# Value pages in four slots, three rounding slots, ranking in PSUM and the key ring over other buffers in a hybrid DeltaNet and MoBA step

## The reference

```
kp = cache_k[i, page_table].reshape(db, past_len, MOBA_HEADS, HEAD_DIM)
gate = jnp.einsum('bhtd,bhnd->bhtn', qh, k_mean)          # k_mean: mean key of each block of 256
_, sel = lax.top_k(gate, n_sel)                            # the best 3 blocks, and the own one
logits = einsum(q, k) * scale - slopes * dist              # ALiBi; others are -1e30
p = softmax(logits); out = einsum(p, v)
```

## Time and profile before

| | |
|---|---|
| median of 3 runs | 1305.23 us (1303.71 to 1305.43) |
| the profiled execution | 1302.96 us, its span 1301.2 us |
| PE busy | 1143.8 us, 88% of the span |
| DVE, ACT, POOL busy | 722.9, 563.0, 294.1 us |
| granted clock of TensorE, mean | 0.937 |
| DMA | 182.62 MB, 140 GB/s over the span |

### The profile page before, as it was taken

The page is one execution under the profiler, slowest core; times in us unless marked ns, Lnnn a source line. Parts: engine busy times, 40 slices in busy tenths (PEclk is TensorE's granted clock), DMA queues, the critical chain, the costliest instruction groups (busy, mean ns, idle before and its releaser), DMA issues.

```text
span 1301.2 us, 20535 instructions
## 1 busy us (share of the span) xinstructions
PE 1143.8 (88%) x7143; PEld 1005.1 (77%) x7143; DVE 722.9 (56%) x1216; ACT 563.0 (43%) x886; POOL 294.1 (23%) x262
## 2 busy tenths in 40 slices
PE   5999689778788788767989999997999799999995
PEld 4999689455455454443889999996999699999994
DVE  4743624566656766642466666345556566666333
ACT  3447301344454555433364444335334554443434
POOL 8201015101454554453220000022101310000011
PEclk9999959888989999985989999998999899999997
DMA  7334100335657666735425345343444244544421
GB/s 229 114 103 157 35 1 1 119 133 186 210 196 242 226 207 215 246 110 162 135 85 174 129 139 181 116 134 118 129 153 149 95 130 147 175 129 135 151 78 40
DMA packets 119124, 182.62 MB, mean 140 GB/s; under 512 B 6128, under 2 KB 59471, under 8 KB 118990
## 3 DMA queue, kind: packets, MB, share of 16 engines
q1 hardware_dynamic: 116274, 173.30, 40.6%
q0 software_dynamic: 2784, 8.47, 2.4%
HBM read 176.12 MB, written 5.63 MB: 140 GB/s over the span
## 4 chain that ended last, share of the span: by engine, by line
PE 46%; ACT 3%; DVE 2%; POOL 1%; issue 0%; DVEq 0%; POOLq 0%
PE bank L1618 46%; POOL xl L617 1%; ACT xres L953 1%; DVE xres L1068 1%; ACT hi L674 1%; ACT xh L674 1%; PE bank L2015 0%; ACT L944 0%; PE bank L2083 0%; DVE xres L1480 0%; DVE hraw L1068 0%; PE bank L2005 0%; DVE lo L1061 0%; DVE lnt L1068 0%; ACT lnt L946 0%
## 5 line engine op out<-in xcount | busy, mean ns | idle before, releaser
L1618 PE MATMUL bank<-xh,hi 128*128 128x320 f32 x1184 | 373.7, 316 | 40.0 <-POOL xl L617 26.4
L1618 PE MATMUL bank<-xl,hi 128*128 128x320 f32 x1184 | 371.3, 314 | 0.0
L1618 PE MATMUL bank<-xh,lo 128*128 128x320 f32 x1184 | 370.9, 313 | 0.0
L1061 DVE TENSOR_TENSOR lo<-raw,hi 128x2048 fp32r<-128x2048 f32 x102 | 241.3, 2366 | 188.6 <-ACT hi L674 188.6
L1618 PEld LDWEIGHTS bank<-xh,hi 128*128 128x128 f32 x1184 | 227.5, 192 | 43.1 <-issue 31.2
L674 ACT ACTIVATE hi<-raw 128x2048 fp32r (+1 forms) x102 | 194.8, 1909 | 107.6 <-PE bank L1618 107.6
L1618 PEld LDWEIGHTS bank<-xl,hi 128*128 128x128 f32 x1184 | 227.5, 192 | 0.1
L1618 PEld LDWEIGHTS bank<-xh,lo 128*128 128x128 f32 x1184 | 227.2, 192 | 0.0
L594 POOL TENSOR_TENSOR lo<-vring,hi 128x1024 fp32r<-128x1024 f32 x60 | 145.0, 2418 | 176.1 <-ACT hi L674 176.0
L1068 DVE TENSOR_TENSOR kTl<-bank,kTh 128x512 fp32r<-128x512 f32 x128 | 88.1, 689 | 103.6 <-ACT kTh L674 101.6
L1618 PE MATMUL bank<-hh,hi 128*128 128x320 f32 x416 | 129.3, 311 | 1.3 <-DVE hraw L1068 1.3
(11 more groups left out here) (376 smaller groups left out, 1500.1 us busy)
## 6 DMA issues: line engine op xcount, KB each, us to landing
raw<-w_up SPq DMA_DIRECT2D x44, 1024.0 KB
kring<-cache_k SPq DMA_DIRECT2D x128, 256.0 KB, 3.7
vring<-cache_v SPq DMA_DIRECT2D x128, 256.0 KB, 3.4
raw<-w_down SPq DMA_DIRECT2D x8, 2048.0 KB
raw<-w_in_mix SPq DMA_DIRECT2D x7, 2048.0 KB
raw<-w_in_sc SPq DMA_DIRECT2D x8, 1024.0 KB
raw<-w_down SPq DMA_DIRECT2D x4, 1536.0 KB
raw<-w_out_mix SPq DMA_DIRECT2D x2, 2048.0 KB
```

The source lines that it names most:

```text
L1061: dve.tensor_tensor(lo[:, p], weight(n)[:, :, 256 * p:256 * p + 256], hi[:, p], ALU.subtract)\
L1618: return pe.matmul(out, lhsT, rhs, start=start, stop=stop, **kw)
```

## The change

- `vring` has four slots of two pages in place of two of four. SP waits and loads by pairs of pages (`load_pair`), two pairs behind each key group; a pair may be loaded when the unit four back has its low part. The number of transfers and of table words is the same.
- Three rounding slots instead of two: `vxh`, `vxl` lie over `kvtok`, the prompt's keys and values, once these are stored. `ROUND_V` is one or two steps earlier. POOL makes all low parts of samples 0 to 6, DVE all of sample 7.
- In the ranking, the block sums are copied into PSUM, and ties, ranks and penalties are kept there; `rk` alone stays in SBUF. Four copies of block maxima become additions with a penalty operand in PSUM.
- The copying of queries and their low part go from DVE to POOL, samples 0 and 1 ahead of the loop.
- `kring` lies over DeltaNet buffers that are dead earlier. SP waits for PE's step o1 and DVE's qg2 for the first group and PE's stS2 for the second, instead of stS3. The first group goes to slot 1.
- Of the four sums for the DeltaNet norm and their logarithms two move into step 0; the prompt's stages move by a step (its values on PE stay at step 13).
- The table `keyb` is made in four operations over 128 partitions, during the inversion, from a small table `spread`, instead of sixteen in step 2 of sample 0.
- `split_lo(S_OUT, 0)` goes from (8, 5) to (7, 11) in DVE's program. The filler stays at (8, 1).

The core of the diff:

```diff
-        c128 = sb("c128", [32, 128], stack=sA)
+        c128 = sb("c128", [P, 128], stack=sA)
         back = sb("back", [32, NPG + 1], stack=sA)
         slope = sb("slope", [32, 1], stack=sA)
         ownb = sb("ownb", [32, 120], stack=sA)
+        keyb = sb("keyb", [P, 512], stack=sA)
+        spread = sb("spread", [P, 5], stack=sA)
...
-        vring = sb("vring", [P, 2, 4, 512], stack=s3)
+        vring = sb("vring", [P, 4, 2, 512], stack=s3)
...
+        kring = sb("kring", [P, 2, 4, 512], stack=s3)
...
+        vxh = sb("vxh", [P, 2, 512], F32R, stack=s3)
+        vxl = sb("vxl", [P, 2, 512], F32R, stack=s3)
...
-        PROMPT = {1: "kv0", 3: "scores", 5: "kv1", 10: "turn", 13: "values"}
+        PROMPT = {0: "sums", 1: "kv0", 4: "scores", 6: "kv1", 11: "turn", 13: "values"}
...
-        ROUND_V = {5: (1, 0), 7: (1, 1), 9: (1, 2), 11: (1, 3), 13: (1, 4), 15: (1, 5), 1: (2, 6), 3: (2, 7)}
-
-        def lo_by_dve(n):
-
-            return n >= VALL - VUNITS and n % 2 == 1
-
-        def lo_ready(eng, n):
-
-            dve_made = sum(lo_by_dve(i) for i in range(n + 1))
-            after(eng, "v_lo", n + 1 - dve_made)
-            after(eng, "v_lo_dve", dve_made)
+        ROUND_V = {3: (1, 0), 5: (1, 1), 8: (1, 2), 10: (1, 3), 12: (1, 4), 14: (1, 5), 0: (2, 6), 2: (2, 7)}
+        LAST_V = VALL - VUNITS
+        vhs = [vh[:, 0], vh[:, 1], vxh[:, :, :]]
+        vls = [vl[:, 0], vl[:, 1], vxl[:, :, :]]
+
+        own_b, pTown_b, den_b = bank[7][0:32, 0:SMP], bank[7][0:SMP, 64:96], bank[7][0:SMP, 96:100]
+        gm_b, tie_b, rank_b, pen_b = (bank[7][0:32, i:i + n] for i, n in
+                                      ((128, NBLK), (136, NBLK * NBLK), (200, NBLK), (208, NBLK)))
...
-            DV.wait(sp_, "stS3")
-            AC.wait(sp_, "oT1")
...
-            def load_pages(ring, cache, landed, n):
-                words = [sp_.value_load(pair[0:1, 2 * n + j:2 * n + j + 1], min_val=0, max_val=POOL * POOL - 1)
-                         for j in range(2)]
-                for j, w in enumerate(words):
-                    for u, x in enumerate((w % POOL, w // POOL)):
-                        sp_.dma_start(ring[:, n % 2, 2 * j + u, :], cache[bass.ds(x, 1)].rearrange("o p h d -> (o p) (h d)"))\
-                           .then_inc(s[f"{landed}{n % 2}"], 16)
+            def load_pair(out, cache, landed, n):
+                w = sp_.value_load(pair[0:1, n:n + 1], min_val=0, max_val=POOL * POOL - 1)
+                for u, x in enumerate((w % POOL, w // POOL)):
+                    sp_.dma_start(out[:, u, :], cache[bass.ds(x, 1)].rearrange("o p h d -> (o p) (h d)")).then_inc(s[landed], 16)
 
             for n in range(4 * NB + 5):
+                if n == 0:
+                    PE.wait(sp_, "o1")
+                    DV.wait(sp_, "qg2")
+                if n == 1:
+                    PE.wait(sp_, "stS2")
                 if n < 4 * NB:
                     after(sp_, "kT_mm", 4 * n - 4)
-                    load_pages(kring, a["cache_k"][0], "k_in", n)
+                    x = (n + 1) % 2
+                    load_pair(kring[:, x, 0:2], a["cache_k"][0], f"k_in{x}", 2 * n)
+                    load_pair(kring[:, x, 2:4], a["cache_k"][0], f"k_in{x}", 2 * n + 1)
                 if n == 5:
                     PE.wait(sp_, "po1")
-                if n >= 5:
-                    lo_ready(sp_, 2 * (n - 5) - 3)
-                    load_pages(vring, a["cache_v"][0], "v_in", n - 5)
+                for m in (2 * n - 10, 2 * n - 9):
+                    if m >= 0:
+                        after(sp_, "v_lo", m - 3)
+                        load_pair(vring[:, m % 4], a["cache_v"][0], f"v_in{m % 4}", m)
...
+            def queries(b):
+                after(pool, "own_mm", b - 1)
+                after(pool, "s_mm", UNITS * (b - 1))
+                pool.tensor_copy(qpf[:, b % 2, :].rearrange("p (h r) -> p h r", r=40)[:, :, 0:NT],
+                                 mbh[:, 0:H, SEQ + NT * b:SEQ + NT * b + NT]).then_inc(s["q_fp"], 1)
+
+            def queries_lo(b):
+                pool.wait_ge(s["q_hi"], b + 1)
+                pool.tensor_tensor(qpl[:, b % 2, :], qpf[:, b % 2, 0:128], qph[:, b % 2, :], ALU.subtract).then_inc(s["q_lo"], 1)
+
+            DV.wait(pool, "rowc")
+            for b in range(2):
+                queries(b)
+                queries_lo(b)
...
-                if lo_by_dve(n):
-                    continue
-                w = n % 2
+            for n in range(LAST_V):
                 pool.wait_ge(s["v_hi"], n + 1)
-                pool.tensor_tensor(vl[:, w], vring[:, n // 2 % 2, 2 * w:2 * w + 2, :], vh[:, w], ALU.subtract)\
-                    .then_inc(s["v_lo"], 1)
+                pool.tensor_tensor(vls[n % 3], vring[:, n % 4], vhs[n % 3], ALU.subtract).then_inc(s["v_lo"], 1)
+                b = n // VUNITS + 2
+                if b < NB and n % VUNITS == 2:
+                    queries(b)
+                if b < NB and n % VUNITS == 4:
+                    queries_lo(b)
...
+            def o_logs(hs):
+                for h in hs:
+                    PE.wait(act, f"oss{h}")
+                    AC.up(act.activation(qg[:, h, :], bank[6 + h % 2][:, 0:TOK], ACT.Ln, scale=1.0 / HD, bias=eps6[:, 0:1]),
+                          f"oln{h}")
...
+                    o_logs((2, 3))
+                    act.preload_act_table(ACT.Exp)
...
-                act.wait_ge(s[f"v_in{n // 2 % 2}"], 64 * (n // 4 + 1))
-                after(act, "v_mm", n - 1)
-                copy(vh[:, n % 2], vring[:, n // 2 % 2, 2 * (n % 2):2 * (n % 2) + 2, :]).then_inc(s["v_hi"], 1)
+                act.wait_ge(s[f"v_in{n % 4}"], 32 * (n // 4 + 1))
+                after(act, "v_mm", n - 2)
+                if n == 2:
+                    act.wait_ge(s["stores"], 16 * 11)
+                copy(vhs[n % 3], vring[:, n % 4]).then_inc(s["v_hi"], 1)
...
+                    for g in range(4):
+                        dve.tensor_copy(spread[32 * g:32 * g + 32, 0:4], back[:, 4 * g:4 * g + 4])
+                        ins = dve.tensor_copy(spread[32 * g:32 * g + 32, 4:5], slope[:, 0:1])
+                    DV.up(ins, "spread")
+                    DV.wait(dve, "spread")
+                    for i in range(4):
+                        dve.tensor_scalar(keyb[:, PAGE * i:PAGE * i + PAGE], c128[:, :], spread[:, i:i + 1], spread[:, 4:5],
+                                          ALU.subtract, ALU.mult)
...
-                    for g in range(NPG):
-                        ins = dve.tensor_scalar(keyb[32 * (g // 4):32 * (g // 4) + 32, PAGE * (g % 4):PAGE * (g % 4) + PAGE],
-                                                c128[:, :], back[:, g:g + 1], slope[:, 0:1], ALU.subtract, ALU.mult)
-                    DV.up(ins, "keyb")
...
-            def queries(b):
-                after(dve, "own_mm", b - 1)
-                for h in range(H):
-                    ins = dve.tensor_copy(qpf[:, b % 2, h, NT * h:NT * h + NT],
-                                          mb[:, TOK * h + SEQ + NT * b:TOK * h + SEQ + NT * b + NT])
-                ins.then_inc(s["q_fp"], 1)
-
-            def queries_lo(b):
-                dve.wait_ge(s["q_hi"], b + 1)
-                tt(qpl[:, b % 2], qpf[:, b % 2], qph[:, b % 2], ALU.subtract).then_inc(s["q_lo"], 1)
...
-                link(dve.tensor_reduce(bm[:, :], sbias[:, c % 2, 0:512].rearrange("p (n k) -> p n k", n=2), AX.X, ALU.max))
+                dve.tensor_reduce(bm[:, :], sbias[:, c % 2, 0:512].rearrange("p (n k) -> p n k", n=2), AX.X, ALU.max)
+                dve.wait_ge(s["summed"], 4 * c + 4)
+                link(dve.tensor_copy(gm_b, gsum[:, :]))
+
+            def ranks(c):
+
+                wins = rk[:, :].rearrange("p (n m) -> p n m", m=NBLK)
+                ties = tie_b.rearrange("p (n m) -> p n m", m=NBLK)
+                gm, gn = mid(gm_b, NBLK), last(gsum[:, :], NBLK)
+                tt(wins, gm, gn, ALU.is_gt)
+                link(tt(ties, gm, gn, ALU.is_equal))
+                link(tt(ties, ties, ltri[:, :, :], ALU.mult))
+                link(tt(wins, ties, wins, ALU.add))
+                link(dve.tensor_reduce(rank_b, wins, AX.X, ALU.add))
+
+            def shifts(c):
+                link(dve.tensor_scalar(pen_b, rank_b, TOPK - 0.5, NEG, ALU.is_gt, ALU.mult))
                 for g in range(4):
-                    dve.tensor_copy(bmax[:, 2 * g:2 * g + 2], bm[32 * g:32 * g + 32, :])
-
-            def ranks(c):
-
-                A, B = [rk[:, i, :].rearrange("p (n m) -> p n m", m=NBLK) for i in range(2)]
-                gm, gn = mid(gsum[:, :], NBLK), last(gsum[:, :], NBLK)
-                dve.wait_ge(s["summed"], 4 * c + 4)
-                tt(A, gm, gn, ALU.is_gt)
-                link(tt(B, gm, gn, ALU.is_equal))
-                link(tt(B, B, ltri[:, :, :], ALU.mult))
-                link(tt(A, A, B, ALU.add))
-                link(dve.tensor_reduce(rank[:, :], A, AX.X, ALU.add))
-
-            def shifts(c):
```

(26 more changed lines are left out.)

147 lines of the change are left out of this document (64 added, 83 removed).

## The result

| | before | changed |
|---|---|---|
| median of 4 runs | 1304.47 us (1302.37 to 1305.43) | 1223.31 us (1222.43 to 1224.06) |
| ratio | | 0.9388 (95%: 0.9370 to 0.9407) |
| span of the profiled execution | 1301.2 us | 1221.9 us |
| mean granted clock | 0.937 | 0.954 |

The change gained 81 us where the prediction had 51 and a range down to 1230. The direction was right, the size was not. What happened is the rival *All waits go* (1229), and a little more. The plain quotient of the two medians is 0.9378, inside the interval of the ratio.

What follows compares the result with a forecast made beforehand. No engine was full; TensorE paused for key pages, delayed by value rounding and DMAs, and for DVE stalled behind POOL. Terms 35 + 3.5 + 14 - 1.5 = 51 us gave 1252, as a median 1254; range 1230 to 1284, likeliest 1238 to 1268.

Steps and rivals of the forecast that it cites:

- All waits go: Rival: TensorE alone sets a sample, 30.3 us; gain 76 us, time 1229; chance 0.12.
- Value slots, rounding slots, earlier rounding, and ranking in PSUM: Steady stretch: earlier value rounding removes 19 of 24.9 us key waits; PSUM ranking and query copies to POOL 9 of 15.3.
- I keep a rest: Steady stretch: of 24.9 us of TensorE's key waits 6 stay and 19 go.
- a third: Steady stretch: share kept of the 15.3 us wait ahead of the first kTh product; 9 us go.
- SP's work stays: Steady stretch: SP keeps 8 groups of 3.38, 27.0 us per sample, with the same number of DMAs and words.
- Clock: Steady stretch: 203.94 us of TensorE work would be 194 at full clock; 7 us gained, bounds 0 and 10.
- Early key ring, start of sample 0: Start: keys no longer decide, first product 6.9 us earlier, half given back; net 3.5 us, from 0 to 8.
- The last sample: Tail: 6.4 us from the filler, 5 from DVE's faster rounding, 2.5 from a POOL wait; together 14, ends 6 and 20.
- The moved split: Loop: 2.27 us of DVE now stand once ahead of a key split; costs 1.5 us, ends 0 and 4.7.
- Keys stay the bound: Rival: keys land after 9.5 us instead of 6.05, a sample takes 36.5; sum 26, time 1279; chance 0.20.
- POOL becomes a gate: Slower rival: queries in POOL's program wait for ACT, delaying value roundings, value DMAs and keys; 1314 us; chance 0.05.
- It does nothing: Rival: SP's order stays, the wait only changes its name, late values eat the tail; 1305 us; chance 0.03.

Runs made afterwards that it cites:

- ranking alone: The kernel before with the ranking in PSUM and nothing else: 1305.6 us, ratio 1.0045.
- late rounding and groups together: Changed kernel with the old rounding steps and value pages again loaded in groups of four: 1281.1 us, ratio 0.9845.
- the groups' return: Changed kernel with both value pairs of an SP iteration waiting for the second pair's condition, so four pages leave together: 1237.0 us, ratio 0.9484.
- late rounding: Changed kernel with the old rounding steps (first unit at step 5, second at 7), three rounding slots kept: 1245.3 us, ratio 0.9574.
- ranking in SBUF: Changed kernel with the ranking back in SBUF (four copies, comparisons and penalties as before): 1254.2 us, ratio 0.9638.

## Why the prediction was wrong, by its own steps

The mechanisms were right and the sizes of their terms were not. Against 51 us of gain stand 79.2 in the profiles. Of the 28.2 too little, 9.8 are idle time that was kept as a rest in the steady stretch, 6.1 the clock term there, 8.7 the clock in the tail, which had no term, 2.1 the start; the last 1.5 were taken off for the moved split, whose cost the measured stretch already holds.

**Value slots, rounding slots, earlier rounding, and ranking in PSUM.** The value path delayed the keys, and the DVE stall was contention with POOL, as forecast. The failed assumption is the way the two were put together. The prediction took 19 of 24.9 and 9 of 15.3 and added them, as if each wait belonged to its edit. The runs show two limits one above the other: ranking alone gave nothing, late rounding and groups together hold 45.6 us of stretch, and ranking is worth 24.6 only where that is gone. In the sum this did little harm, since both went. What did harm are the rests: "I keep a rest" of 6 for keys, and "a third" of the DVE wait because DVE had more work in steps 0 to 4 than TensorE. 1.4 and 1.0 stayed. Idle time fell by 37.8 us, 10 more than the 28 forecast.

"SP's work stays" was right in count and missed a point: by the program a wait per pair lets SP do its reads and first transfers before it stands, and the groups' return cost 10.5 us of stretch.

**Clock.** 7 was taken, measured is 203.94 - 190.82 = 13.1. The bound of 10 came from busy time times mean clock (194), which was no lower bound: the same products at clock 1.00 took 190.8. What the missing 3 us are, no run shows. In the runs with pauses TensorE's busy time stands at 193 to 210. From before to changed, the pauses removed gave back a third of themselves once more (13.1 for 37.8); the single edits range from a quarter (late rounding, 4.5 for 16.6) to over a half (ranking in SBUF, 8.7 for 15.9). This term and the rests make the 16 us by which the steady stretch was missed.

**Early key ring, start of sample 0.** First product forecast 6.9 earlier, measured 8.2 (262.50 to 254.32); first turn 3.5, measured 5.6. Inside the ends of 0 to 8. The giving back was right in kind, 2.6 instead of 3.5. The estimate of 2.5 us for the two samples' queries rested on no row; POOL makes them from 251.27 to 253.43, 2.2 us.

**The last sample.** 14 forecast, 22.7 measured, above the upper end of 20. TensorE's idle time in the tail fell from 17.9 to 3.9 us, which is the 14 forecast, and its parts fit too (6.4, 2.7 and 4.9 of waits gone, against 6.4, 2.5 and 5). Its busy time for the same 100 products fell from 31.8 to 23.1, at a clock of 0.87 instead of 0.66, and that 8.7 is the whole miss: the prediction noted the 0.66 and gave it no term. By segments against the earlier trace rows: up to the filler 8.1 to 1.0 us; filler to the first value of the last sample 15.7 to 10.1; these values up to the projection 25.9 to 15.9. The first is the 6.4 forecast, and a little. The second lost the 2.5 forecast for POOL's rounding and, unforeseen, as much again by clock: the filler's products run at 0.31 throughout, where 17 of the 24 took 0.42 to 0.63. The third gave 10 where 5 was taken. The waits for roundings in it fell by 4.9, as forecast; but the pace of 1.75 us a unit was that of products of 0.63 us, and from 528.7 on they take 0.39.

**The moved split.** 1.5 forecast; TensorE waits 1.02 us at 507.48 for kTl. Undone it costs 9.5 net, not 4.9. The prediction said that the split would wait for a POOL operation whenever it comes second. The rows agree, and the next POOL operation waits in turn:

```profile
502.19 2.39 POOL L608 TENSOR_TENSOR lo<-vring,hi 128x1024 fp32r<-128x1024 f32 x1 [2.44 <-ACT hi L692]
503.86 2.87 DVE L1084 TENSOR_TENSOR lo<-raw,hi 128x2048 fp32r<-128x2048 f32 x1
505.38 3.59 POOL L608 TENSOR_TENSOR lo<-vring,hi 128x1024 fp32r<-128x1024 f32 x1 [0.80 <-ACT hi L692]
```

The split takes 2.87 instead of 2.27 us, POOL's rounding 3.59 instead of 2.4.

**The rivals.** *Keys stay the bound* fell: transfers land 3.4 us after issue at the median (3.7 before) while 273 GB/s move. The Trainium skill (DMA: Bandwidth & Descriptors, Bandwidth) asks for 1 MiB per transfer for three quarters of the peak; these of 256 KB kept the DMA engines busy 0.85 of the time, and TensorE waited 1.4 us for keys. That does not contradict the page, since 273 GB/s stay under the 341 that the prediction took from it for 1 MB, measured there on loads issued from GpSimd. *POOL becomes a gate* fell: moving the queries from POOL back to DVE changes nothing, and the key wait is 1.4 us in all. *It does nothing* is right for the ranking alone (1.0045), not for the whole. *All waits go* had the right picture at 30.3 us per sample (30.1 measured) and was given 0.12, on the argument "DVE's steps 0 to 4" that no row had shown to bind without the stall. It too had no term for the clock in the tail.

## What to carry to other kernels

When two waits of one engine sit in the same stretch, ask what each becomes if the other goes: work out each resource's own time for a period, and take the largest, not the sum of parts. Here that meant TensorE 30, SP 27 and the DMA engines below (busy 0.85 of 30.1), with both stalls gone, and no rest without a row that shows it. Give every stretch with pauses a clock term of its own, the tail too, and bound it by the fastest seen pace of the same products (value products follow each other every 0.23 us at clock 1.00 and every 0.43 at 0.50), not by busy time times mean clock. When an operation is moved into another engine's busy time, ask what waits behind it at that step: of DVE's stalls 11 us cost nothing in one place, and 24 us lengthened the stretch by 24.6 in another. A queue that works in order, near its own limit, should wait as late and for as little as it can.

## What the runs showed of the hardware

- Two tiny DVE comparisons with both operands in SBUF took 4.14 us, spanning two POOL operations of 2.4 back to back, where alone they take 0.34: the stall can be had twice in one chain. With one operand in PSUM they took 0.20 and 0.21 beside POOL.
- A DVE copy of 128x32 elements from SBUF to SBUF took 1.99 us beside a POOL operation, and the same copy on POOL 0.21. A DVE split of 2.27 us took 2.87, and the POOL operation begun during it 3.59 instead of 2.4: the blocking goes both ways.
- After a pause of 6.68 us, 128x320 products took 0.47 us until 523.3 and 0.31 from 523.6, 5.5 us after the restart; the granted clock was 0.50 and then 1.00. In the changed kernel a pause of 1.94 us, with a few short products ahead of it, was enough: clock 1.00 over the filler, 0.50 from 522.5 to 528.3, 1.00 from 528.7.
- With page loads of 256 KB issued by SP alone, the DMA engines moved 273 GB/s over 195.6 us.
- Equal idle time did not mean equal speed: 42.6 us of pauses went with 203.9 us of busy time; 41.5 us in the kernel before with the ranking alone, nearly all of it in twelve waits for keys, with 209.9.
